# Modulation vectors by VectorE's multiply-and-sum in place of band matmuls, with the heads' norm and turn split

## The reference, cut to what matters

```python
def adaln(c, w, b):
    m = jax.nn.silu(c.astype(jnp.float32)) @ w + b      # c: (1, 1024), w: (1024, 3072)
    shift, scale, gate = jnp.split(m, 3, axis=-1)
    return shift[:, None, :], scale[:, None, :], gate[:, None, :]
```

## Time and profile before

| | |
|---|---|
| median of the runs | 1982.12 us |
| span of the profiled execution | 1980.0 us |
| TensorE busy | 1919.8 us, 97% |
| VectorE busy | 689.7 us, 35% |
| ScalarE busy | 372.2 us, 19% |
| GpSimd busy | 115.0 us, 6% |
| mean data rate | 244 GB/s |

### The profile page before, as it was taken

How to read it: one execution, slowest core, us unless ns; L and a number is a source line. 1 busy time by engine, 2 the same in 40 slices (tenths; PEclk the granted TensorE clock), 3 DMA queues, 4 the chain that set the end, 5 groups by cost and what they waited for, 6 DMA issues and landing times.

```text
span 1980.0 us, 28488 instructions
## 1 busy us (share of the span) xinstructions
PE 1919.8 (97%) x11940; PEld 1070.5 (54%) x11940; DVE 689.7 (35%) x1472; ACT 372.2 (19%) x776; POOL 115.0 (6%) x98
## 2 busy tenths in 40 slices
PE   7999999999998999999989988999999999999998
PEld 6577866577865765776756544232323233333332
DVE  3364414354413573434449943010101010101112
ACT  3322102222103232234320012010101010101011
POOL 0000010000010000000016620000000000000000
PEclk9999999999999999999999998999999999999999
DMA  9255574264673316533323135999989999999993
GB/s 359 94 218 208 222 296 170 95 245 182 243 290 128 128 43 246 191 159 128 127 106 126 45 149 202 365 378 376 374 374 375 374 369 382 366 379 364 389 368 143
DMA packets 44037, 483.98 MB, mean 244 GB/s; under 512 B 5108, under 2 KB 6772, under 8 KB 10328
## 3 DMA queue, kind: packets, MB, share of 16 engines
q1 hardware_dynamic: 39136, 471.73, 59.2%
q10 hardware_dynamic: 4248, 9.07, 1.3%
q0 software_dynamic: 576, 2.10, 0.3%
HBM read 479.07 MB, written 10.10 MB: 247 GB/s over the span
## 4 chain that ended last, share of the span: by engine, by line
PE 88%; DVE 6%; DMA 3%; issue 1%; ACT 1%; ACTq 1%; POOL 0%; DVEq 0%; SPq 0%
PE bank L921 20%; PE bank L579 14%; PE bank L951 12%; PE bank L874 8%; PE bank L886 4%; PE bank L738 3%; PE bank L571 3%; PE bank L564 3%; PE bank L744 3%; PE bank L592 2%; PE bank L1000 2%; DMA arena<-bias_rows 1%; PE bank L1095 1%; PE bank L560 1%; PE bank L1028 1%; PE bank L935 1%
## 5 line engine op out<-in xcount | busy, mean ns | idle before, releaser
L921 PE MATMUL bank<-arena 128*32 128x512 f32 x4096 | 457.3, 592 | 0.0
L579 PE MATMUL bank<-arena 128*128 128x256 f32 x1408 | 313.3, 382 | 0.0
L921 PEld LDWEIGHTS bank<-arena 128*32 128x32 f32 x4096 | 136.1, 110 | 300.3 <-issue 300.3
L579 PEld LDWEIGHTS bank<-arena 128*128 128x128 f32 x1408 | 265.5, 190 | 54.2 <-issue 15.8
L951 PE MATMUL bank<-arena 128*32 128x512 f32 x2112 | 238.2, 595 | 0.0
L2077 DVE TENSOR_TENSOR arena<-arena,bank 128x256 f32<-128x256 f32 x64 | 27.0, 421 | 562.1 <-ACT arena L1447 511.6
L874 PE MATMUL bank<-arena 128*128 128x256 f32 x704 | 153.7, 379 | 0.1
L874 PEld LDWEIGHTS bank<-arena 128*128 128x128 f32 x704 | 133.6, 190 | 21.8 <-issue 4.1
L951 PEld LDWEIGHTS bank<-arena 128*32 128x32 f32 x2112 | 62.9, 109 | 133.3 <-issue 132.7
L1447 ACT ACTIVATE arena<-bank 128x256 f32<-128x256 f32 x64 | 24.6, 385 | 517.5 <-PE bank L921 517.4
L2323 POOL TENSOR_TENSOR arena<-arena 128x512 f32<-128x512 f32 x64 | 81.3, 1270 | 293.4 <-DVE arena L2131 290.9
(11 more groups left out here) (446 smaller groups left out, 1894.4 us busy)
## 6 DMA issues: line engine op xcount, KB each, us to landing
arena<-in_wgu SPq DMA_DIRECT2D x88, 2048.0 KB, 10.2
arena<-in_w SPq DMA_DIRECT2D x46, 2048.0 KB, 8.1
arena<-in_wdn SPq DMA_DIRECT2D x88, 1024.0 KB, 9.6
arena<-in_modw SPq DMA_DIRECT2D x24, 2048.0 KB, 9.3
arena<-in_wf SPq DMA_DIRECT2D x11, 3072.0 KB, 10.4
arena<-in_flt_deltas ACTq DMA_DIRECT2D x2, 1024.0 KB, 11.7
slot_rows<-arena ACTq DMA_DIRECT2D x7, 192.0 KB, 3.5
cst<-in_consts SPq DMA_DIRECT2D x1, 1162.0 KB, 7.7
```

The lines of the kernel that those rows point to most:

```text
L579: ins = mm(bank[b][:, j * S:(j + 1) * S], w[:, col:col + P], hT[:, k, :], start=(k == 0), stop=(k == KT - 1))
L921: ins = mm(bank[w % 2][32 * j:32 * j + 32, :], hTe[:, k, TOK * b:TOK * b + TOK], wslot[SLOT[c]][:, k, :], start=(k == 0), stop=(k == KT - ...
```

## The change

TensorE's steps `modmul` and `mod`, ScalarE's copies for them and GpSimd's sums are removed. The host lays the modulation weights out turned: partition p of a chunk holds the 1024 weights of four outputs, one after the other. `c` is loaded to all partitions (512 KB) and ScalarE makes silu(c) of it in place. A new step `modulate` on VectorE multiplies 128x1024 weights by silu(c) and sums them into one column of `mods`, four operations a chunk in direct succession. SyncE's load into the place of a modulation chunk waits for that sum (`mod_sum`). The chunks are placed behind n8, n11, n13, n15, n16, n18, n20, n22, n23, n26, n30 and n32, ahead of what the table `after` hangs in there. VectorE's step `heads_out` ends with the norm; the turned heads are taken in a step of their own behind n21.

```diff
-GROUPS_1 = 36 + MOD_CHUNKS
+GROUPS_1 = 36
...
+    parts = {}
+    for at, n in enumerate([8]*4+[11]*4+[13]*4+[15]*4+[16]*4+[18]*4+[20]*4+[22]*4+[23]*4+[26]*4+[30]*4+[32]*4):
+        parts.setdefault(n, []).append((at // 4, at % 4))
     out = [("norm", 0, 0), ("lam_in", 0, 0)]
     for n, step in enumerate(g):
-        c, h = step[1:]
-        if c >= 4 and h == 0:
-            m = c - 4
-            out.append(("modmul", m, 0))
-        if step == g[-1]:
-            out.append(("mod", 0, 0))
         out.append(step)
+        out += [("modulate", m, q) for m, q in parts.get(n, [])]
         out += after.get(n, [])
...
-LOAD_END = [max(n for (name, c, _), n in GROUP.items() if name == {"w": "proj", "m": "modmul"}[kind] and c == chunk) + 1
+LOAD_END = [max(n for (name, c, _), n in GROUP.items() if c == chunk) + 1 if kind == "w" else chunk + 1
             for kind, chunk in LOADS]
...
             sp.dma_start(ev[:, :], a["vec2"]).then_inc(sm["ev_landed"], 16)
+            sp.dma_start(silu_c, a["c"].partition_broadcast(P)).then_inc(sm["ev_landed"], 16)
...
-                    sp.wait_ge(sm["grp_ps"], l * GROUPS_1 + LOAD_END[n - RING])
+                    if LOADS[n - RING][0] == "w":
+                        sp.wait_ge(sm["grp_ps"], l * GROUPS_1 + LOAD_END[n - RING])
+                    else:
+                        sp.wait_ge(sm["mod_sum"], l * MOD_CHUNKS + LOAD_END[n - RING])
...
-                                act.wait_ge(sm["ev_landed"], 16)
-                                F(band[:, :, 31:32], ev[:, E_C:E_C + 8].unsqueeze(2), ACT.Silu).then_inc(sm["c_ready"], 1)
+                                act.wait_ge(sm["ev_landed"], 32)
+                                F(silu_c, silu_c, ACT.Silu).then_inc(sm["c_ready"], 1)
...
+                    elif name == "modulate":
+                        at = PLACE[("m", c)]
+                        if h == 0:
+                            dve.wait_ge(landed[at % RING], l * (16 * LOADS_1 // RING) + 16 * (at // RING + 1))
+                        if l + c + h == 0:
+                            dve.wait_ge(sm["c_ready"], 1)
+                        w = ring[at % RING][:, h * D:(h + 1) * D]
+                        col = (l * MOD_CHUNKS + c) * 4 + h
+                        ins = v.tensor_tensor_reduce(out=w, in0=w, in1=silu_c, scale=1.0, scalar=0.0, op0=ALU.mult, op1=ALU.add,
+                                                     accum_out=mods[:, col:col + 1])
+                        if h < 3:
+                            link(ins)
+                        else:
+                            ins.then_inc(sm["mod_sum"], 1)
+                            dve.wait_ge(sm["mod_sum"], l * MOD_CHUNKS + c + 1)
...
                         ins.then_inc(sm["on_ready"], 1)
+                        dve.wait_ge(sm["on_ready"], l + 1)
+                    elif name == "heads_turn":
                         for i in range(2):
                             out_of(l, ("proj", ZA, i))
```

More of the change, by code:

```diff
@@ L106 @@
 STEPS = layer_steps()
-GROUP = {step: n for n, step in enumerate(s for s in STEPS if s[0] in ("proj", "modmul"))}
+GROUP = {step: n for n, step in enumerate(s for s in STEPS if s[0] == "proj")}
 assert len(GROUP) == GROUPS_1
 YSQ = {GROUP[("proj", WO0 + i, t)]: 2 * t + i + 1 for t in range(TT) for i in range(2)}
-LOAD_END = [max(n for (name, c, _), n in GROUP.items() if name == {"w": "proj", "m": "modmul"}[kind] and c == chunk) + 1
+LOAD_END = [max(n for (name, c, _), n in GROUP.items() if c == chunk) + 1 if kind == "w" else chunk + 1
             for kind, chunk in LOADS]
@@ L260, in model @@
         tmp = view(att + 3072, 2, 512)
-        modsum = view(att + 4096, 512)
-        band = view(att + 4608, KT, 63)
-        modout = view(att + 5120, 2, 512)
+        silu_c = view(att + 4096, D)
         biasr = view(LOW + 3072, 4, TT, S)
@@ L357, in model @@
                 on_ready yt_ps ya_ready
-                macc_used mod_ps mod_in mask_landed gb_in gb_ps gb_ready
+                mod_sum mask_landed gb_in gb_ps gb_ready
                 gla_ps gla_act gla_in gla_done cl_ready fsc_ps fsc_ready fpr_ready fw_ready ft_ps fpt_ready fva_ps
@@ L537, in _ @@
                         if l:
-                            pe.wait_ge(sm["macc_used"], l)
+                            pe.wait_ge(sm["ya_ready"], l)
                         mm(bank[7][:, 0:2], ones, small[:, 0:2], start=True, stop=True).then_inc(sm["lam_ps"], 1)
@@ L581, in _ @@
                         ins.then_inc(sm["grp_ps"], 1)
[L582 to L601, removed]
                     elif name == "bias" and l == 0:
@@ L1266, in _ @@
                         ins.then_inc(free[n % 2], 1)
[L1267 to L1276, removed]
                     elif name == "f_sine":
@@ L1560, in _ @@
             link(v.memset(small[:, :], 0.0))
-            link(v.memset(band.rearrange("p a b -> p (a b)"), 0.0))
             v.memset(small[:, 95:96], 1e-6).then_inc(sm["x_ready"], 1)
@@ L1825, in _ @@
             link.restart()
-            dve.wait_ge(sm["macc_used"], DEPTH)
-            dve.wait_ge(sm["ev_landed"], 16)
+            dve.wait_ge(sm["ev_landed"], 32)
             link(v.tensor_tensor(mods[:, :], mods[:, :], ev[:, E_MB:E_MB + 96], ALU.add))
@@ L2301, in _ @@
             link = Chain(pool, sm["pool_chain"])
[L2303 to L2313, removed]
             pool.wait_ge(sm["xt_ps"], 16)
@@ L2425 @@
     mw = _np.stack([i[k][0] for k in ("e_mod_mix_w_2", "e_mod_ffn_w_2", "o_mod_mix_w_2", "o_mod_ffn_w_2")])
-    g["modw"] = mw.reshape(4, KT, P, 3, 2, 512).transpose(0, 3, 4, 2, 1, 5).reshape(24, P, CH)
+    g["modw"] = mw.reshape(4, D, 6, 4, P).transpose(0, 2, 4, 3, 1).reshape(24, P, CH)
+    g["c"] = i["c_2"][0]
     mb = _np.stack([i[k][0] for k in ("e_mod_mix_b_2", "e_mod_ffn_b_2", "o_mod_mix_b_2", "o_mod_ffn_b_2")])
```

## The result

The changed kernel takes 1990.76 us (median of 5 runs, 1984.47 to 1993.02) against 1982.12 (1980.96 to 1983.53): ratio 1.0037, interval 1.0021 to 1.0054. Ten more runs of it beside 19 of the kernel before gave 1988.53 against 1983.60, ratio 1.0026 (1.0010 to 1.0042). It is slower, by 5 to 9 us; 1981 was forecast, with 1970 to 1990 as the range. The profiled execution is the fastest of the first five, with a span of 1982.6 us against 1980.0.

A forecast was written before the change was run, and what follows sets the result against it. TensorE was taken to bound the kernel. A layer gains 24.2 less 17.9 of waits and 5.1 of half clock, 1.2; two gain 2.4, the start costs 1.2: net -1.2, 1981 us, range 1970 to 1990.

The forecast's parts named there:

- The operation's cost: VectorE's multiply-and-sum on 1024 elements: 1.27 us each, 5.07 a chunk, 61 us a layer; bounds 752 and 1284 ns.
- GpSimd's share: GpSimd's 24 additions and copies go, giving VectorE's chain about 1.05 us in three places of a layer.
- The five waits: New TensorE waits in each layer, four for VectorE and one for weights, summing to 17.9 us a layer.
- wait 2: TensorE waits for VectorE before the inverse transform L674, behind n14: 2.7 us a layer.
- wait 3: TensorE waits for VectorE before the turn L654, behind n15: 5.4 us, a head's turn of 0.4 inside.
- wait 4: TensorE waits before n24 for PA's weights, queued behind m8's load, which waits for m6's sum: 0.9 us.
- The clock: Half clock on TensorE's matmuls behind new waits: 1.7 us behind each of three waits, 5.1 us a layer.
- waits 1, 3 and 5: Waits for VectorE before head 0's turn (4.1 us), turn L654 (5.4) and output projection (4.8), each charged 1.7 of clock.
- The start: The 512 KB copy of c in the saturated DMA phase delays the bias rows' landing: 1.2 us.
- The load rival: Weights queued behind modulation loads in SyncE's in-order queue land later, 3.6 us more a layer: 1988 us, chance 0.25.
- The clock rival: Clock stays up behind the new waits, or most are shorter; price -10.2, 1971 us, chance 0.15.
- the dearer operation: VectorE's operation costs more than its row, 4.8 us per 0.1 us; 1984 us at 1284 ns; chance 0.07.

The follow-up runs named there:

- best: The `both` kernel with the copy of c issued behind w4's load, as in c_late; 1941.06 us, ratio 0.9785 against the kernel before.
- both: Changed kernel with modulation sums behind the attention's parts, chunks m2 and m10 later, and weights w6 to w12 loaded ahead of modulation loads; 1940.20 us, ratio 0.977.
- w_first: Changed kernel with SyncE issuing the loads of w6 to w12 ahead of the modulation load that stood before each; 1982.93 us.
- filled: Changed kernel with 12 idle matmuls a layer inside three TensorE waits (head 0's turn, turn after n15, output projection); 1978.37 us, ratio 0.9973.
- heads_joined: Changed kernel with the heads' norm and turn again in one VectorE step; 2011.55 us (two runs).
- c_late: Changed kernel with the copy of c issued behind w4's load instead of in the first 20 us; 1985.38 us in 11 runs.

## Why the prediction was wrong, point by point

**What bounds the kernel, and what is removed: right.** TensorE was the path; with nearly all waits mended 41.6 of 48.4 us show in `best`, and in the layers of `both` 43.2.

**The operation's cost: right**, 1225 ns, 1.27 from start to start. The near end of the bounds held, and the ends at 752 and 1284 ns were not reached.

**GpSimd's share: right.** L1711 is at 353 ns throughout, and the sum of waits fits with it (it would be 3.1 us a layer more without).

**The five waits: right in place and sum, the sum in part by luck**, 17.7 and 18.0 against 17.9. In layer one wait 2 was not for VectorE: w7 was 1.7 us late and nothing was left behind it, so waits 2 and 3 were 1.0 smaller each and wait 4 1.8 larger. Wait 4 was mis-sized, 2.7 and 1.8 for 0.9. The term behind it is the landing of a pair of loads. I took 12.4 us from a single landing and a rate; from SyncE's issue at 237.06 to the start of PA at 250.72 it is 13.7, in layer two 12.7, for w7 12.9 and 12.7. Wait 3 was 1.0 and 0.5 smaller. In w_first, where w7 isn't late, it is 4.9 in both layers: from L657's start at 163.71 VectorE needs the 17.3 us of the forecast, but TensorE 12.4 and not 11.9. So w7's lateness explains the other 0.5 of layer one.

**The clock: the step that failed in the profiled run.** The term stands in the sum as 1.7 us behind waits 1, 3 and 5, 10.2 in all; it was 8.6 and 6.1, together 14.7. Behind the three waits charged it was 11.6, mostly because wait 3 cost 2.6 and 2.2: it is two waits with a head's turn of 0.7 us between them. The rest are the waits for weights of layer one, w7's and PA's, which I had called absorbed and short and charged nothing; they cost 1.7 and 1.5. The error of 4.5 us is more than the whole gain of 2.4 that I had left. That the slow stretches are the clock is shown by filled; that its 10.2 us equal my 10.2 is luck, for its trace gains 13.7 in the layers, behind more waits than I had charged.

**The start: right in size by luck.** 1.2 was forecast and 1.3 seen in the profiled run, but there a wait of 2.1 us behind the constants' load stands where the forecast had a longer wait for the bias rows. Nor is it a fixed shift: with the early copy the step that needs the bias rows began between 47.0 and 53.9 us. Moving the copy brought 1.7 to 3.5 us, by the pair that is compared, and neither pair is clear of noise.

**From the span to the median: not in the sum at all.** The profiled run was the fastest of five, 6.3 us under the median. I had carried the difference of the spans over to the medians as it stood, as if the changed kernel's median lay 2.1 us above its profiled span like that of before; it lies 8.2 above. These 6.1 us are the larger part of the 9.8 by which 1981 was missed, the 3.8 of the spans (-1.2 forecast, 2.6 seen) the smaller. The second trace, 6.3 us above the first, puts 1.5 at the start, 2.0 in the layers, 1.7 of them half clock behind PA's wait, and 2.8 in the second block.

**The rivals.** The load rival (1988, chance 0.25) is the nearest in number, which is luck in the main, and part of it happened: pairs landed 0.3 to 1.3 us later than I took, PA's wait grew and pulled the clock down in layer one. But w8 and w9 were never late in the changed kernel's trace, and w_first brings 5.6 us where the rival had charged 7.2 on top of the forecast's 1.8 of wait 4. So it is a part and not the cause. The clock rival had the wrong sign, the dearer operation did not occur. With 1990.76 the time lies 0.8 above the range. I had let each case end where its own terms ended; the two that came true together, clock and loads, and the spread at the start, were not added.

The ten runs of the second series gave 1988.5, within the range, but 7.5 us from the forecast and on the other side of the kernel before; what is settled is that the change is no gain as it stands (1.0037 and 1.0026, both intervals above 1), and why.

What makes 2.8 us between runs in the second block stays open; a wait for weights of 2.1 instead of 0.3 us is part of it, and it is seen with and without the sum's placing.

## What to carry to other kernels

Work that moves from the bound engine to an idle one is free only at the places where nobody waits behind it: the average busy share doesn't tell where. One walk along the engine's list, from each wait back, gave the waits for VectorE to within 0.5 us where no late load lay ahead of them and within 1.0 elsewhere; the waits for loads it missed by up to 1.8. Look for every queue that the moved work now gates: here SyncE's in-order loads tied weights to VectorE, and neither the better placing alone (1993) nor the better load order alone (1983) showed what both did (1940). Count for every new wait on TensorE of some microseconds the half clock behind it, also where the wait is for data: here 1.2 to 3.1 us behind those above 3 us, and 0 or about 1.6 behind those of 1.4 to 2.8. Carry no difference of two profiled spans over to medians without a look at the spread of both kernels.

## What the runs showed of the hardware

Idle matmuls inside three of TensorE's waits in each layer made the kernel 9 to 10 us faster; in the windows behind waits 1 and 3 of layer one the granted clock was 1.00 with them and 0.59 and 0.50 without. The price of one wait varied from 0 to 3.1 us (the most in heads_joined, where PA's matmuls took 30.93 us behind a wait of 13.3, and 27.87 where nothing slowed them), and below 3 us its length alone did not tell it: 1.47 us for w7 in layer two cost nothing (the group behind it took 7.14 us), 1.69 in layer one cost 1.7 (8.83), and 1.80 in layer one of c_late cost nothing (7.14); for PA 2.71 us cost 1.5 and, in c_late, 2.62 nothing. Two loads of 2 MB issued together needed 12.7 to 14.3 us until the engine that waited for the second began, 5.2 to 6.8 more than the 7.5 of one alone. And 512 KB more in the first 20 us, in whose second half the DMA share was 1.00 to 1.02, went with a step that waits for small loads of another queue and began 0.3 to 7.6 us later (at 46.4 to 46.7 without it, at 47.0 to 53.9 with it).
